# Last two weight units of the MLP's second output half taken tile by tile, with fewer constant products at two layer ends

## What is computed

```python
# first block, for tokens and, in its first layer, for the context
y = (silu(h @ w_gate) * (h @ w_up)) @ w_down
x = x + g_f * y
# second block
g, u = jnp.split(h @ w_gate_up, 2, axis=-1)
y = (silu(g) * u) @ w_down
x = x + g_f * rms_norm_2(y, ffn_norm_post)
```

## Time and profile before

| | |
|---|---|
| median of 3 runs | 3339.8 us (3338.57 to 3352.28) |
| profiled execution, its own time | 3341.87 us |
| span of its trace | 3340.0 us |
| PE busy | 3196.0 us, 96% |
| DVE busy | 1952.8 us, 58% |
| ACT busy | 1128.5 us, 34% |
| mean granted TensorE clock | 0.987 |

### The profile page before, as it was taken

The page is one execution under the profiler, slowest core; times in us unless marked ns, Lnnn a source line. Parts: engine busy times, 40 slices in busy tenths (PEclk is TensorE's granted clock), DMA queues, the critical chain, the costliest instruction groups (busy, mean ns, idle before and its releaser), DMA issues. The chain is left out here.

```text
span 3340.0 us, 44487 instructions
## 1 busy us (share of the span) xinstructions
PE 3196.0 (96%) x17810; PEld 2611.5 (78%) x17810; DVE 1952.8 (58%) x3410; ACT 1128.5 (34%) x1987; POOL 175.6 (5%) x171
## 2 busy tenths in 40 slices
PE   5999998999999999999999999999999999999998
PEld 4988777888888898777877777677877777678886
DVE  3676656746464435667555667756545677643334
ACT  3134643111112424642222544542222535442222
POOL 0000000000000000000000036000000054000000
PEclk9999999999999999999999999999999999999999
DMA  5442113423231221136544231045543221023332
GB/s 206 146 131 84 39 45 94 156 82 114 95 114 58 68 70 50 56 101 208 160 139 148 61 95 57 13 127 189 164 150 115 85 78 45 26 76 98 92 101 76
DMA packets 316029, 335.19 MB, mean 100 GB/s; under 512 B 11896, under 2 KB 219312, under 8 KB 315824
## 3 DMA queue, kind: packets, MB, share of 16 engines
q1 hardware_dynamic: 315824, 332.35, 31.9%
HBM read 328.63 MB, written 3.67 MB: 99 GB/s over the span
## 5 line engine op out<-in xcount | busy, mean ns | idle before, releaser
L2175 DVE TENSOR_TENSOR weights_low<-weights,weights_high 128x1024 fp32r<-128x1024 f32 (+5 forms) x416 | 489.0, 1177 | 762.9 <-ACT weights_high L1535 760.8
L1535 ACT ACTIVATE weights_high<-weights 128x1024 fp32r<-128x1024 f32 (+5 forms) x416 | 420.4, 1012 | 1263.4 <-PE banks L685 799.7
L1305 PE MATMUL banks<-h_high,weights_high 128*128 128x512 f32 (+1 forms) x1760 | 656.5, 373 | 20.9 <-DVE h_low L2187 12.8
L1305 PE MATMUL banks<-h_low,weights_high 128*128 128x512 f32 (+1 forms) x1760 | 649.5, 369 | 0.0
L1305 PE MATMUL banks<-h_high,weights_low 128*128 128x512 f32 (+1 forms) x1760 | 649.0, 369 | 0.0
L685 PE MATMUL banks<-weights_high,h_high 128*128 128x512 f32 (+4 forms) x1360 | 512.7, 377 | 15.0 <-DVE h_low L2187 10.4
L685 PE MATMUL banks<-weights_high,h_low 128*128 128x512 f32 (+4 forms) x1360 | 501.1, 368 | 0.0
L685 PE MATMUL banks<-weights_low,h_high 128*128 128x512 f32 (+4 forms) x1360 | 499.7, 367 | 0.0
L1305 PEld LDWEIGHTS banks<-h_high,weights_high 128*128 128x128 f32 x1760 | 333.0, 189 | 87.8 <-DVE h_low L2187 14.6
L1305 PEld LDWEIGHTS banks<-h_high,weights_low 128*128 128x128 f32 x1760 | 332.6, 189 | 56.2
L1305 PEld LDWEIGHTS banks<-h_low,weights_high 128*128 128x128 f32 x1760 | 333.1, 189 | 52.8
(11 more groups left out here) (403 smaller groups left out, 3807.0 us busy)
## 6 DMA issues: line engine op xcount, KB each, us to landing
projected<-in_w_mod SPq DMA_DIRECT2D x44, 1024.0 KB, 6.6
weights<-in_w_gate_up SPq DMA_DIRECT2D x88, 512.0 KB, 3.8
weights<-in_w_down SPq DMA_DIRECT2D x80, 512.0 KB, 3.8
extra<-in_w_mod SPq DMA_DIRECT2D x36, 1024.0 KB, 6.6
weights<-in_w_in SPq DMA_DIRECT2D x48, 512.0 KB, 3.7
weights<-in_w_gate SPq DMA_DIRECT2D x44, 512.0 KB, 4.6
weights<-in_w_up SPq DMA_DIRECT2D x44, 512.0 KB, 3.9
weights<-in_w_mod SPq DMA_DIRECT2D x32, 512.0 KB, 4.0
```

The source lines that it names most:

```text
L1305: mm = pe.matmul(bank[:, 0:cnt], wt[:, k, :], x[:, k, a - GOFF:a - GOFF + cnt], start=(k == 0 and q == 0), stop=(k == KD - 1 and q == 2))
L1535: act.activation(WH[s_ % 2][:, 0:k * n], slots[j % LAND][:, 0:k * n], ACT.Copy).then_inc(S["w_high"], 1)
L2175: dve.tensor_tensor(WL[s_ % 2][:, 0:k * n], slots[split_of[s_] % LAND][:, 0:k * n], WH[s_ % 2][:, 0:k * n].bitcast(F32), ALU.subtract).the ...
```

## The change

`product` gets a flag `by_tile`, set for the second half of the last part in every layer. With it the last two units, (18,20) and (20,22), are taken together: for each tile first the matmuls of the one, then those of the other. Both units are asked for ahead of the first tile. The release of unit (18,20) comes with its matmuls on the last tile. The numbers of constant products become 4, 6 and 9.

```diff
-                for k, kn in order:
+                for k, kn in order[:-2] if by_tile else order:
                     wh, wl = next_unit()
...
+                if by_tile:
+                    (ka, kb), (kc, kd) = order[-2:]
+                    if ready:
+                        pe.wait_ge(S[low], max(ready[kb - 1], ready[kd - 1]))
+                    both = [(ka, kb, next_unit()), (kc, kd, next_unit(1))]
+                    for t in tt:
+                        at = slice(t * PT - off[1], (t + 1) * PT - off[1])
+                        for k, kn, (wh, wl) in both:
+                            for kk in range(k, kn):
+                                for q, (x, wt) in enumerate(((ah, wh), (ah, wl), (al, wh))):
+                                    mm = pe.matmul(out_banks[t][:, 0:n], x[:, kk - off[0], at], wt[:, kk - k, :],
+                                                   start=False, stop=(kk == k_last - 1 and q == 2))
+                            if k == ka and t == tt[-1]:
+                                part_used(mm)
+                        mm.then_inc(B.filled, 1)
+                    release.append((B.name, B.filled_so_far()))
...
-                    product(GH, GL, OUT_T, (m0, GOFF), 512, m0, m1, lambda i: "d", ready)
+                    product(GH, GL, OUT_T, (m0, GOFF), 512, m0, m1, lambda i: "d", ready, by_tile=(half, m1) == (1, KF))
...
-                warm(11 if second else 4 if with_ctx else 9)
+                warm(9 if second else 4 if with_ctx else 6)
```

More of the change, by code:

```diff
@@ L662, in part_used, with product @@
                 release.append(("unit_part", mine["part"]))
-            def product(ah, al, tt, off, n, k0, k1, by, ready=None, B=B, after=None, behind=None, low="emptied_dve", between=None, order=None, by_block=True):
+            def product(ah, al, tt, off, n, k0, k1, by, ready=None, B=B, after=None, behind=None, low="emptied_dve", between=None, order=None, by_block=True, by_tile=False):
                 out_banks = {}
```

## The result

| | before | after |
|---|---|---|
| median | 3347.1 us (13 runs, 3337.8 to 3352.3) | 3356.8 us (13 runs, 3352.7 to 3360.4) |
| ratio | | 1.0028, 95% interval 1.0019 to 1.0037 |
| profiled execution, span | 3341.9 us, 3340.0 | 3357.5 us, 3355.6 |

The change makes the kernel slower by 9.4 us (6.4 to 12.4), worked out from the ratio. That is within 0.5%, but clear of no change, and the time lies above the range of 3338 to 3353. The three runs of before that were shown had a median of 3339.8; thirteen have 3347.1. Runs of before scatter over 15 us.

What follows compares the result with a forecast made beforehand. PE was taken as the bound, busy 3196 of 3340 us. The wait's 11.1 us less 7.3 given back makes +3.8 on the 3339.8 median, 3343.6; one dip of 1.6 gives 3345.2 us, range 3338 to 3353.

Steps and rivals of the forecast that it cites:

- The new wait: Before tile 0 of the last two units, PE waits for both splits: 2.77 us per layer, 11.1 us in all.
- Tile by tile, and `warm`: At the layer ends, tiles ending 12 matmuls apart and fewer constant products give back 7.3 us.
- The clock: Behind the four new gaps of PE, one short dip to half clock, +1.6 us.
- Rival 4: A short dip in all four new gaps: 3350.0 us; chance 0.15.
- How the numbers follow: For the whole kernel: range 3338 to 3353 us; chance 0.94 within 0.5%, 0.05 above 3356.5, 0.01 below 3323.1.
- rival 1: Long stretches at half clock behind each of the four new gaps: 3361.6 us; chance 0.04.
- rival 2: The split is ready at the last two units, so PE does not stop: -7.3 us, 3332.5 us; chance 0.03.
- rival 3: Next layer's start changes speed: 3348 us if layer two's turns slow, 3342 if layer three's turns fast; chance 0.15.

Runs made afterwards that it cites:

- e3: The changed kernel with a third pair of buffers for the last unit's split halves; measured 0.9971, -9.7 us against the kernel before.
- e9: The changed kernel with the second wait moved ahead of unit (20,22) on tile 0, same matmul order; measured 0.9985, -5.0 us against the kernel before.
- e10: The changed kernel with unit (18,20) running one tile ahead of (20,22), two buffers as before; measured 0.9986, -4.7 us against the kernel before.
- e8: The third-buffer kernel e3 with constant products in the older gaps of the MLP; measured 0.9960, -13.4 us against the kernel before, from five runs.
- e4: The changed kernel with three constant products ahead of the two waits for the split halves; measured 1.0014, +4.7 us against the kernel before.
- e1: The changed kernel with the 4, 9 and 11 constant products of before; measured 1.0034, +11.4 us against the kernel before.
- e2: The kernel before with 4, 6 and 9 constant products and nothing else changed; measured 1.0000 against the kernel before.
- e7: The kernel before with a third pair of buffers for the last split and nothing else; measured 0.9991, -3.0 us against the kernel before.

## Why the prediction was wrong

The forecast of 3345.2 us missed the measured 3356.8 by 11.6. The level that it started from was 7.3 us too low, and the change itself cost some 4 us more than the +5.4 forecast. The first is the anchor, the second the term for the clock.

*The new wait.* Right. I said 2.63 us later and 0.14 of slower first matmuls. In layer one, at full clock, the stretch grew by 2.80 us. What limited it was the two buffers, as e3, e9 and e10 show from three sides.

*Tile by tile, and `warm`.* Right, and its size too. Without the wait (e3, e8) the ends moved by 0, -2.6, -1.7 and -2.8 us; I had 0, -2.6, -1.7 to -1.9 and -2.8. With the wait and no dip (e4) they moved by +2.8, +0.25, +1.15, where I had +2.8, +0.2 and +0.8 (or +1.1). The 1.26 us for the barrier taken over from layer two was the wrong choice: layer three takes 1.49 behind PE both before and after (after: 2623.60, then 2625.09). Layer four is 0, as said, if its two dips are taken off.

*The clock: this step failed.* I took "one short dip among the four new gaps, +1.6", because one of three older gaps before such matmuls had one. A gap of 2.56 us was followed by a dip in 3 of 4 places in the changed kernel's trace and in 4 of 4 in e1's. That is 7 of 8, or 5.7 us on four. The price of one dip, 1.6, was right; their number was not. The three rows I had chosen were gaps of 1.99, 2.02 and 3.43 us, none near 2.6. Two more waits for `weights_low` of that kind, at 2445 and 3311 us, had no dip in the trace of before either, so the kind of matmul told nothing. The trace of before had three nearer ones, at 66, 2129 and 2866 us, and low clock came behind all three. That at 2129 I set aside since its matmuls were small; that at 66 us I overlooked, and its matmuls are those of `product`, with 428 columns:

```profile
66.19 0.43 PE L685 MATMUL banks<-weights_high,h_high 128*128 128x428 f32 x1 [2.45 <-DVE h_low L2187]
```

The granted clock was 0.57 from 68 to 72 us.

Rival 4, four dips, was the mechanism that came, and by my own working it cost +10.2 us against before (3.8 + 6.4), with 9.4 measured. I had given it 0.15. That the two numbers lie so close is partly luck: the changed kernel's trace has three of the four dips, and two more behind older gaps that had none in the trace of before. Filling the gap, fully or by a third, took back 4.7 and 7.7 us, so the dips were a matter of this gap.

The Trainium skill (page "TensorE: Matmul & The Clock Gate", section "Why this matters for your kernels") warns of idle gaps between bursts of matmuls that are longer than these. Read as it stands it lets one expect no dip behind 2.56 us. Here the measurement decides against it: a dip followed in 7 of 8 places. Behind the longer gap of 3.43 us in layer two it followed in only 5 of 11 profiles.

*How the numbers follow.* The second fault is that I anchored on the median of three runs, 3339.8, and on the profiled 3341.9. Runs of before have their median between 3347.1 and 3348.7 in four jobs. Those 7 us are more than half of the 11.6 by which my 3345.2 missed 3356.8. The ratio was the better quantity: I said +5.4 us, it was +9.4. The range did take in the scatter of 3338.6 to 3352.3, but its upper end, 3353, is the highest run of before with nothing of the forecast's shift added.

*The rivals.* Long dips (rival 1) did not come. No wait (rival 2) was out for the changed kernel, and became e3. Colder starts (rival 3): in the changed kernel's trace the start of layer three had one dip more, in its first matmuls; behind layer three the 16 transposes took the fast 1.98 us, not 3.33, and the dip came in the matmuls after them. This adds 2.0 us to the profiled difference. It doesn't need the shorter `warm`: e1, with the long one, has low clock at the start of layer three too (0.66 from 1887 to 1892 us). Whether the shorter `warm` makes it likelier stays open, since e2's trace shows a cold start there and its median no loss.

*Still open.* Several kernels (e3, e7, e9) are 2.5 to 3.5 us better in the median than the sum of their layer ends. With low clock behind 83 of 160 gaps of 1.9 to 2.3 us, such sums can shift by what comes elsewhere, but I have no run that shows it.

## What to carry to other kernels

Where two buffers are used in turn, asking for both at once puts the whole refill of the second on the path. Ask for the second where its first use is: six matmuls' distance turned +9 us into -5 here. An order that drains its outputs evenly is worth what the consumer's queue was, and the constant work that covered that queue has to shrink with it, since it holds the barrier.

Price a gap of TensorE as its length plus the dip behind it. Look first at gaps of the same *length* in the trace, all of them, but the length alone doesn't decide (next section): several traces, or a run with the gap filled, tell what a given place does. Filling a third of the gap was enough here. And take the level of a kernel from more than three runs when these differ by more than the effect.

## What the runs showed of the hardware

In the thirteen traces, gaps of TensorE from 1.6 to 2.6 us behind the first 60 us, counted with those followed within 5 us by a stretch at the lower level:

| gap, us | followed by low clock |
|---|---|
| 1.6 to 1.7 | 5 of 74 |
| 1.9 to 2.3 | 83 of 160 |
| 2.4 to 2.6 | 42 of 45 |

Nine of the 160 began with the clock low already. Of 40 gaps of 2.9 to 3.3 us 38 had low clock behind them, 10 of these from before the gap. The low stretch behind the gaps in the MLP mostly costs 1.6 to 1.7 us at a time, once 2.5.

Length isn't all that counts. Of the 45 in the last line 33 are three places of the program, low each time, eight are the new gaps of the changed kernel and e1, seven of them with a dip, and four are starts of layer four. Five gaps of the MLP, all waits for `weights_low` before matmuls of the same shape, stand in eleven of the traces:

| place (time before), gap | followed by low clock |
|---|---|
| 869 us, 1.99 us | 10 of 11 |
| 1707 us, 2.02 us | 0 of 11 |
| 2445 us, 2.02 us | 4 of 11 |
| 3311 us, 1.95 us | 8 of 11 |
| 1852 us, 3.43 us | 5 of 11 |

So one length went from never to nearly always by its place, and the longest fared no worse than the shorter ones. What makes the difference between the places no run here shows. I had not expected that, nor that the same place in the same program goes one way in one execution and the other in the next: the gap in layer four at 3311 us had no dip in the trace of before and one in that of after. That is also a likely part of the 15 us over which the runs of before scatter; the runs do not show it by themselves.
